# A row of norm factors multiplied into the MLP activations where the up banks are emptied, in place of a per-token scalar on the second projection's output

## The reference

```python
def rms_norm(x, g):
    y = xf * lax.rsqrt(jnp.mean(xf * xf, axis=-1, keepdims=True) + NORM_EPS)
    return (y * g).astype(x.dtype)
...
        u = rms_norm(h, mlp_pre_g[l])
        a = jnp.square(jax.nn.relu(u @ w_up[l]))
        h = h + rms_norm(a @ w_down[l], mlp_post_g[l])
```

## Time and profile before

| | us |
|---|---|
| median of three runs | 610.77 |
| the profiled execution, whole | 610.47 |
| its span, first to last instruction | 608.5 |
| PE busy | 594.7 (98%) |
| DVE busy | 296.7 (49%) |
| ACT busy | 268.0 (44%) |
| POOL busy | 100.3 (16%) |

### The profile page before, as it was taken

The page is one execution under the profiler, slowest core; times in us unless marked ns, Lnnn a source line. Parts: engine busy times, 40 slices in busy tenths (PEclk is TensorE's granted clock), DMA queues, the critical chain, the costliest instruction groups (busy, mean ns, idle before and its releaser), DMA issues.

```text
span 608.5 us, 8201 instructions
## 1 busy us (share of the span) xinstructions
PE 594.7 (98%) x2992; PEld 500.5 (82%) x2992; DVE 296.7 (49%) x587; ACT 268.0 (44%) x564; POOL 100.3 (16%) x167
## 2 busy tenths in 40 slices
PE   7999999999999999999999999999999999999996
PEld 7988898887777788998888888888888888888884
DVE  3458582788788408535433534334242332423345
ACT  5563262788898424264425344252321313213132
POOL 1153200346798101120000000000000000000011
PEclk9999999999999999999999999999999999999999
DMA  8441412000220084004232242323223131232303
GB/s 305 128 129 57 169 70 69 1 1 1 71 71 1 6 306 139 0 1 139 69 113 94 73 134 69 111 96 122 86 76 131 69 130 77 77 130 69 104 16 122
DMA packets 32826, 55.24 MB, mean 91 GB/s; under 512 B 3232, under 2 KB 21408, under 8 KB 32800
## 3 DMA queue, kind: packets, MB, share of 16 engines
q1 hardware_dynamic: 31760, 54.90, 26.9%
q10 hardware_dynamic: 1040, 0.00, 0.1%
HBM read 52.80 MB, written 2.10 MB: 90 GB/s over the span
## 4 chain that ended last, share of the span: by engine, by line
PE 92%; DVE 3%; ACT 2%; issue 1%; DMA 1%; SPq 0%; DVEq 0%; POOLq 0%; POOL 0%; ACTq 0%
PE bank L913 30%; PE bank L914 29%; PE bank L915 29%; PE bank L1083 2%; DVE pT_lo L635 1%; ACT probs L501 1%; DVE bank L767 1%; DMA x_sb<-in_x 1%; PE bank L919 1%; PE bank L1020 1%; PE bank L952 1%; DVE kT_lo L635 0%; PE bank L1036 0%; ACT uT_hi L389 0%; ACT pT_hi L389 0%
## 5 line engine op out<-in xcount | busy, mean ns | idle before, releaser
L913 PE MATMUL bank<-uT_hi,w_hi 128*128 128x512 f32 (+1 forms) x280 | 104.0, 371 | 0.0
L914 PE MATMUL bank<-uT_lo,w_hi 128*128 128x512 f32 (+1 forms) x280 | 103.8, 371 | 0.0
L915 PE MATMUL bank<-uT_hi,w_lo 128*128 128x512 f32 (+1 forms) x280 | 103.8, 371 | 0.0
L913 PE MATMUL bank<-w_hi,a_hi 128*128 128x512 f32 x256 | 99.7, 389 | 0.1
L914 PE MATMUL bank<-w_lo,a_hi 128*128 128x512 f32 x256 | 99.6, 389 | 0.0
L915 PE MATMUL bank<-w_hi,a_lo 128*128 128x512 f32 x256 | 99.6, 389 | 0.0
L635 DVE TENSOR_TENSOR w_lo<-w_raw,w_hi 128x2048 fp32r<-128x2048 f32 (+1 forms) x17 | 38.4, 2261 | 111.8 <-ACT w_hi L389 111.8
L389 ACT ACTIVATE w_hi<-w_raw 128x2048 fp32r<-128x2048 f32 (+2 forms) x25 | 37.0, 1490 | 118.7 <-PE bank L915 117.9
L638 DVE SCALAR_TENSOR_TENSOR w_lo<-w_raw,g_up,w_hi 128x256 fp32r<-128x256 f32 x128 | 52.1, 480 | 48.3 <-ACT w_hi L389 48.3
L599 ACT ACTIVATE relu<-bank 128x512 f32<-128x512 f32 x32 | 19.1, 598 | 98.2 <-PE bank L915 98.2
L322 POOL TENSOR_SCALAR stat<-stat 128x1 f32<-128x1 f32 x8 | 1.9, 239 | 363.9 <-ACT junk_post L414 363.9
(11 more groups left out here) (127 smaller groups left out, 944.6 us busy)
## 6 DMA issues: line engine op xcount, KB each, us to landing
w_raw<-in_w_up SPq DMA_DIRECT2D x16, 1024.0 KB, 5.2
w_raw<-in_w_down SPq DMA_DIRECT2D x16, 1024.0 KB, 4.8
w_raw<-in_w_in SPq DMA_DIRECT2D x6, 1024.0 KB, 5.8
w_raw<-in_w_out SPq DMA_DIRECT2D x4, 1024.0 KB, 4.8
x_sb<-in_x SPq DMA_DIRECT2D x8, 256.0 KB, 5.9
h_sb<-in_x SPq DMA_DIRECT2D x4, 512.0 KB, 4.9
out<-h_sb SPq DMA_DIRECT2D x8, 256.0 KB, 2.0
w_raw<-in_w_in SPq DMA_DIRECT2D x2, 416.0 KB, 5.0
```

The lines of the kernel that those rows point to most:

```text
L913: nc.tensor.matmul(out, lh, rh, start=start, stop=False)
L914: nc.tensor.matmul(out, lh, rl, start=False, stop=False)
L915: return nc.tensor.matmul(out, ll, rh, start=False, stop=stop)
```

## The change

The factor r (no longer r * r) is brought to the up projection's output. It must lie along the free dimension there, the same on every partition. So TensorE transposes it: four transposes of the column r of a token tile, broadcast to 128 columns, fill bank 4 (L1180 of the changed kernel) and count `rT_full`; they stand between half B of block 2 and block 3, and wait for `rstd` of the four tiles. ScalarE copies the bank into a new SBUF tile `r_row` (`row_ready`), ahead of its `up_step`. VectorE waits for that once, and now empties each up bank itself: max(z, 0) * r_row into `relu[m]`, one instruction, counted in `relu_c`. ScalarE squares `relu[m]` into `act_sb`, counted in `a_ready`. At the end the scale of y's squares and the factor in `scaled` go, and GpSimd's four r * r with them.

```diff
--- before.py
+++ after.py
@@ -137,6 +137,7 @@
         post_g = sb("post_g", [P, D])
         un = sb("un", [P, D])
         junk_post = sb("junk_post", [P, D], BF16)
+        r_row = sb("r_row", [P, S])
 
         ps = [ctx.enter_context(nc.psum_tensor(f"bank{b}", [P, TOP], F32)) for b in range(8)]
 
@@ -181,6 +182,7 @@
         y_s = sem("y_s")
         h_ready = sem("h_ready")
         up_full, relu_c, a_ready = sem("up_full"), sem("relu_c"), sem("a_ready")
+        rT_full, row_ready = sem("rT_full"), sem("row_ready")
         ah, al = sem("ah"), sem("al")
         out_done = sem("out_done")
 
@@ -313,7 +315,7 @@
                 ins.then_inc(pool_step, 1)
                 pool.wait_ge(pool_step, own[0])
 
-            def rms(norm, t, n, n_sq, parts=1, by=None, squared=False):
+            def rms(norm, t, n, n_sq, parts=1, by=None):
 
                 s = stat[:, norm, t, :]
                 add = EPS
@@ -324,9 +326,9 @@
                 pool.wait_ge(sq, n_sq)
                 step(nc.gpsimd.tensor_scalar(s[:, 2:3], s[:, parts - 1:parts], 1.0 / n, add, ALU.mult, ALU.add))
                 last = nc.gpsimd.tensor_tensor(s[:, 3:4], s[:, 2:3], half, ALU.pow)
-                if by is not None or squared:
+                if by is not None:
                     step(last)
-                    last = nc.gpsimd.tensor_tensor(s[:, 3:4], s[:, 3:4], s[:, 3:4] if squared else by, ALU.mult)
+                    last = nc.gpsimd.tensor_tensor(s[:, 3:4], s[:, 3:4], by, ALU.mult)
                 last.then_inc(rstd, 1)
 
             for t in range(NT):
@@ -366,7 +368,7 @@
             for t in range(NT):
                 rms(3, t, D, 3 * NT + 2 * t + 2, parts=2)
             for t in range(NT):
-                rms(4, t, D, 5 * NT + t + 1, squared=True)
+                rms(4, t, D, 5 * NT + t + 1)
             for t in range(NT):
                 rms(5, t, D, 6 * NT + 2 * t + 2, parts=2)
 
@@ -593,11 +595,12 @@
                         act.wait_ge(up_full, i * 4 + 2 * j)
                         mlp_hi(1 - j, i * 2 + (UP_CH + j + 1), not (last and j == 1))
                     for m in range(2):
-                        act.wait_ge(up_full, i * 4 + (2 * j + m + 1))
-                        if not (first and j == 0):
-                            act.wait_ge(a_ready, i * 4 + (2 * j + m - 1))
-                        nc.scalar.activation(relu[:, m, :], ps[2 * j + m][:, :], ACT.Relu).then_inc(relu_c, 1)
-
+                        act.wait_ge(relu_c, i * 4 + (2 * j + m + 1))
+                        nc.scalar.activation(act_sb[:, bass.ds(i * 4 + (2 * j + m), 1), :], relu[:, m:m + 1, :],
+                                             ACT.Square).then_inc(a_ready, 1)
+
+            act.wait_ge(rT_full, 1)
+            nc.scalar.copy(r_row[:, :], ps[4][:, :]).then_inc(row_ready, 1)
             up_step(0, first=True)
             act.wait_ge(a_ready, 2)
             hi_part(a_hi[0][:, :, :], act_sb[:, 0:2, :]).then_inc(ah, 1)
@@ -619,7 +622,7 @@
                     down_hi(j, i * 2 + j)
             for t in range(NT):
                 act.wait_ge(rstd, 4 * NT + t + 1)
-                y_squares(5, NT + t, t, stat[:, 4, t, 3:4])
+                y_squares(5, NT + t, t)
 
 
         @block.vector
@@ -846,7 +849,7 @@
 
             halves = [0]
 
-            def scaled(norm, t, n_sq, n_rstd, n_g, by=None):
+            def scaled(norm, t, n_sq, n_rstd, n_g):
 
                 dve.wait_ge(g_post_in, n_g)
                 for b in range(2):
@@ -855,12 +858,7 @@
                         dve.wait_ge(h_ready, halves[0] - 1)
                     halves[0] += 1
                     dve.wait_ge(sq, n_sq + b)
-                    if by is None:
-                        last = nc.vector.tensor_tensor(un[:, w], ps[2 * t + b][:, :], post_g[:, w], ALU.mult)
-                    else:
-                        last = nc.vector.scalar_tensor_tensor(out=un[:, w], in0=ps[2 * t + b][:, :], scalar=by,
-                                                              in1=post_g[:, w], op0=ALU.mult, op1=ALU.mult)
-                    last.then_inc(y_s, 1)
+                    nc.vector.tensor_tensor(un[:, w], ps[2 * t + b][:, :], post_g[:, w], ALU.mult).then_inc(y_s, 1)
                 dve.wait_ge(rstd, n_rstd)
                 for b in range(2):
                     w = slice(TOP * b, TOP * b + TOP)
@@ -880,14 +878,17 @@
                     if not (first and j == 0):
                         mlp_lo(1 - j, i * 2 + (UP_CH + j + 1), not (last and j == 1))
                     for m in range(2):
-                        dve.wait_ge(relu_c, i * 4 + (2 * j + m + 1))
-                        nc.vector.tensor_tensor(act_sb[:, bass.ds(i * 4 + (2 * j + m), 1), :], relu[:, m:m + 1, :],
-                                                relu[:, m:m + 1, :], ALU.mult).then_inc(a_ready, 1)
+                        dve.wait_ge(up_full, i * 4 + (2 * j + m + 1))
+                        if not (first and j == 0):
+                            dve.wait_ge(a_ready, i * 4 + (2 * j + m - 1))
+                        nc.vector.scalar_tensor_tensor(out=relu[:, m, :], in0=ps[2 * j + m][:, :], scalar=0.0,
+                                                       in1=r_row[:, :], op0=ALU.max, op1=ALU.mult).then_inc(relu_c, 1)
 
             def down_a(j, c):
                 dve.wait_ge(ah, c + 1)
                 lo_part(a_lo[j][:, :, :], act_sb[:, bass.ds(c * 2, 2), :], a_hi[j][:, :, :]).then_inc(al, 1)
 
+            dve.wait_ge(row_ready, 1)
             up_step(0, first=True)
             down_a(0, 0)
             with dve.Fori(1, NF // 4 - 1) as i:
@@ -903,7 +904,7 @@
                 for j in range(2):
                     down_lo(j, i * 2 + j)
             for t in range(NT):
-                scaled(5, t, 6 * NT + 2 * t + 1, 5 * NT + t + 1, 32, stat[:, 4, t, 3:4])
+                scaled(5, t, 6 * NT + 2 * t + 1, 5 * NT + t + 1, 32)
 
 
         @block.tensor
@@ -1174,6 +1175,10 @@
             pe.wait_ge(ul, 4 * NT)
             for bank in range(3):
                 up_block(bank, bank // 2, bank % 2, B).then_inc(up_full, 1)
+            pe.wait_ge(rstd, 5 * NT)
+            for t in range(NT):
+                last = nc.tensor.transpose(ps[4][:, P * t:P * t + P], stat[:, 4, t, 3:4].to_broadcast([P, P]), ident[:, :])
+            last.then_inc(rT_full, 1)
             up_block(3, 1, 1, slice(0, S)).then_inc(up_full, 1)
             with pe.Fori(1, NF // 4) as i:
                 for j in range(2):
```

## The result

The changed kernel takes 616.64 us (median of four runs: 616.55, 616.57, 616.71, 617.56) against 610.75 us before (the three runs of above and a fourth): a ratio of 1.010, 95% interval 1.0083 to 1.0118. It is slower by 5.9 us. The forecast's sign and range held (613.9 to 617.1 us), but its likeliest case, 615.1 us, did not: the time is that of the second case, the stall and the fallen clock together, 616.5 us. That the range held is owed to its taking in that case. The profiled execution took 616.55 us, with a span of 614.7 us.

A forecast was written before the change was run, and what follows sets the result against it. TensorE, nearly always busy at top clock, was taken to bound the kernel. A 4.45 us delay of block 4 less 0.09 us at the end gave +4.36 us: 615.1 us against 610.77 us, range 613.9 to 617.1 us.

The forecast's parts named there:

- its likeliest case: Block 4 stalls about 4.4 us for chunk 16's weights with TensorE at full clock: 615.1 us, chance 0.67.
- the second case: Rival: TensorE's clock also falls in the new gap ahead of block 4, costing 1.4 us more: 616.5 us, chance 0.19.
- What bounds the kernel: TensorE, busy for 594.7 of 608.5 us at top clock, bounds it; anything that keeps it waiting is a loss.
- The wait of TensorE for r: Ahead of block 3, the transposes' wait for norm 4's last factor costs nothing, with 4.9 us of cover.
- The transposes: Four transposes ahead of block 3 take 0.60 us and hold back the next matmul by 0.40 us.
- The chain to chunk 16: Transposes, copy, two products, second square, hi part and lo part in sequence make block 4 late by 4.45 us.
- either bound: Ends for VectorE's product with an immediate, which the trace lacked: 0.48 us (256 columns, SBUF) and 2.29 us (2048 columns).
- Chunk 17: Next weights, for block 6: ready at about 289.7 us, wanted at 291.1 us; cover 1.4 us, no second stall.
- the later chunks: Each later up chunk's chain takes 7.9 us of the 10.88 us of two blocks: hidden, with 3 us of cover.
- the passage to the down projection: Last product and square replace last relu and square, 0.75 + 0.60 us for 0.60 + 0.69 us: costs nothing.
- The end: The last square of y loses its pointer scale: 0.09 us gained; VectorE's cheaper product counts for nothing.
- the prediction's own sign: Listed signs of being wrong; one was the clock's column dropping ahead of 290 us.

The follow-up runs named there:

- the filled gap: The changed kernel with 56 small matmuls into an unused bank between block 3 and the wait for chunk 16: 615.05 us.
- the split ahead: The changed kernel with the split of chunk 16 (hi and lo part) moved ahead of the copy of r_row and the first products: 610.98 us against 610.83 us.
- the exchange alone: The kernel before with VectorE emptying up banks by max and product with a row of ones, ScalarE squaring, no transposes or copy: 610.70 us against 610.83 us.
- the unused copy: The kernel before with only the four transposes and ScalarE's copy of r_row added, the row used by nothing: 615.61 us median, ratio 1.0075.

## Why the prediction was right, and where it was wrong

*What bounds the kernel* was right. TensorE had no slack, so that a stall at block 4 came out whole at the end: the last square starts at 609.04 us instead of 602.77 us, 6.27 us later. That is 0.15 us from before the transposes, 0.35 us for the transposes and 0.09 us more for the first matmul behind them, 3.94 us from where the next matmul was due (276.14 + 0.23 = 276.37 us) to 280.31 us, about 0.1 us for the first matmul there, and 1.59 us of clock: 6.22 us, and 0.05 us are left.

*The wait of TensorE for r* cost nothing, as said. *The transposes* held back the next matmul by 0.35 us (270.47 to 270.82 us), and 0.09 us by its fill, for 0.40 us forecast. No cost of the broadcast operand shows.

*The chain to chunk 16* was right in its order, its members and its sum. With the 0.15 us that the execution was late by then, the copy was to start at 271.10 us (it did at 271.11), the products at 271.73 (271.73), the hi part at 273.66 (273.59), and TensorE at 280.28 us (280.31). The pair of products took 1.29 us instead of 1.40 us: the form with an immediate takes 688 ns, less than the 749 ns of L861 with its pointer scalar, and nearer to it than to either bound. That the sum came out to 0.03 us is in part luck: the cheaper pair of products (0.11 us) was set off by a second square that takes 0.04 us more to the next start (0.54 us), and by a step from the lo part to TensorE of 0.15 us (280.16 to 280.31 us) in place of 0.03 us. The gap was forecast with 3.78 us and measured with 3.78 us. The stall's own price, from the filled gap against the split ahead, is 615.05 - 610.98 = 4.07 us; forecast were 4.05 us beyond the transposes (4.45 - 0.40).

*Chunk 17, the later chunks, the passage to the down projection*: no further gap, as said, and the exchange alone changed nothing in the time. *The end*: 0.09 us, as said.

*The step that failed* is the choice between the first two cases, and in it the argument against the fall of the clock, "the gap is longer by no more than 0.14 us". It took the 3.6 us of idle time ahead of the fall at the end of the trace for the length at which the clock falls. The runs show no such length: with 2.76 us it fell in four of five runs, with 2.65 us in two of five, with 3.78 and 4.26 us in all eight, and with 0.91 us in none of ten, by their times (the gaps are those of the profiled executions, and in the one of 2.65 us small matmuls stand ahead of it, so that it differs in more than its length). In the changed kernel it fell some 0.6 us after TensorE had started again. One fall in one trace gives no threshold. By the prediction's own sign, the clock's column dropping ahead of 290 us, its likeliest case was wrong. The sum was right for the case that it described and lacked a term of 1.6 us. Its price, estimated as 1.4 us, was near by luck: the clock column reads 1.00 over the first matmuls of the program, so that their wide spacing isn't shown to be a fallen clock, and the low stretch lasted from about 280.9 to 284.3 us and not 2.84 us.

The rival that was given only 0.19 is the one that held. What the prediction cites beside it from the Trainium skill (TensorE: Matmul & The Clock Gate, section "HAM oscillation — how this bites in real kernels"), that the next group of matmuls starts cold, once for each gap, held in part: the clock fell with the gap of 3.78 us in all four runs, by their times, but the next group started at the full clock, and the fall came about 0.6 us behind its start.

Why the same gap lets the clock fall in one execution and not in another, no run here shows; nothing in the instructions differs between a run of 614.22 and one of 615.60 us. The Trainium skill (TensorE: Matmul & The Clock Gate, section "What's actually happening") says that the monitor looks at activity in a window that runs freely and does not start with the kernel. Two outcomes of one kernel agree with that, without showing it.

The parts of the loss are 0.15 us with the order mended, the transposes less what the end gives back, which a measurement can't tell from nothing; 4.07 us for chunk 16 behind the wait; and 1.59 us for the clock: 610.83 + 0.15 + 4.07 + 1.59 = 616.64 us. These are differences of medians, each to the next, so they add up of themselves. What speaks for the two large parts is that the rows give nearly the same: 3.94 and 0.1 us for the wait, and 1.59 us for the spacing.

## What to carry to other kernels

Where an engine works in program order, ask of each new wait what is queued behind it for someone else; here a 0.6 us copy, unused in one of the experiments, held back the weights of the engine that bounds the kernel, and moving the split ahead of it took the loss away. On a kernel bound by TensorE, price a new gap of the lengths seen here, 2.65 us and up, with the clock as well, as a likely case and not as a rival, and test it by filling the gap with matmuls that nobody reads. A mean of runs with two outcomes hides this: look at each run's mean clock.

## What the runs showed of the hardware that was not expected

- The granted clock fell after a gap and not only in it: at about 280.9 us, when TensorE had been busy again since 280.31 us. The first two matmuls ran at the full clock, the third stood 0.37 us ahead of the next, and from there they stood 0.43 us apart. With the unused copy it fell inside the gap, close to 279 us with TensorE starting at 279.41 us, and that fall cost 1.38 us and not 1.59 us.
- The same program falls or not: 614.22 or 615.6 us with a gap of 2.76 us, 614.8 to 615.0 or 616.3 to 616.6 us with one of 2.65 us.
- With gaps of 3.78 and 4.26 us there is a third outcome, 0.6 to 1.0 us above, in one run of four and three of four, at a mean clock of 0.992 to 0.993. Its cause is open.
- The form max-and-multiply with an immediate out of PSUM takes 688 ns for 512 columns, as a plain product of two tensors does (L859, 688 ns), while the form with a pointer scalar takes 749 ns (L861).
